# Hybrid retention and HGRN2 layer on eight cores: block 1's x by TensorE, the residual by an accumulating DMA, the sample tile last

## The reference

```python
h = _rmsnorm(x, g_pre)
u = jnp.einsum('btd,de->bte', h, w_in)            # w_in 1024 x 4096
rq, rk, rv, rg, hq, hf, hi, hg = jnp.split(u, cuts.tolist(), axis=-1)   # 512 columns each
rq = _rotary(_heads(rq, RET_HEADS), pos)
rk = _rotary(_heads(rk, RET_HEADS), pos) * (RET_DK ** -0.5)
hq = jax.nn.silu(_heads(hq, HG_HEADS))
f = lb + (1.0 - lb) * jax.nn.sigmoid(_heads(hf, HG_HEADS))
logf, hk = jnp.log(f), 1.0 - f
o_r, o_h, S_ret, S_hg = _run_mixers(S_ret, S_hg, rq, rk, rv, hq, hk, hv, logf, log_gamma)
o = jnp.concatenate([jax.nn.silu(rg) * _merge(_head_norm(o_r)),
                     jax.nn.silu(hg) * _merge(_head_norm(o_h))], axis=-1)
y = jnp.einsum('bte,ed->btd', o, w_out)           # w_out 1024 x 1024
return x + _rmsnorm(y, g_post), S_ret, S_hg
```

## Time and profile before

| | us |
|---|---|
| three runs | 386.45, 387.47, 388.98 |
| median | 387.47 |
| profiled execution | 388.32 |
| its span, slowest core (core 7) | 386.8 |
| span of the fastest core (core 0) | 381.1 |
| PE / DVE / ACT / POOL busy, core 7 | 358.8 / 255.6 / 180.9 / 205.5 |

### The profile page before, as it was taken

How to read it: one execution, slowest core, us unless ns; L and a number is a source line. 1 busy time by engine, 2 the same in 40 slices (tenths; PEclk the granted TensorE clock), 3 DMA queues, 4 the chain that set the end, 5 groups by cost and what they waited for, 6 DMA issues and landing times.

```text
span 386.8 us, 8100 instructions; the slowest of 8 cores (381.1 to 386.8 us)
## 1 busy us (share of the span) xinstructions
PE 358.8 (93%) x2339; PEld 188.1 (49%) x2339; DVE 255.6 (66%) x554; ACT 180.9 (47%) x563; POOL 205.5 (53%) x277
## 2 busy tenths in 40 slices
PE   8599799998988989997999999999999999999982
PEld 8554354455544444453545454545455554554541
DVE  0316565827889998969395949386849467486364
ACT  2431245557767546471636253446262533646341
POOL 8525541545775785774283645375837436347130
PEclk9989899999999999998999999999999999999988
DMA  7999999996488476964537335432233443233217
GB/s 177 204 177 165 202 163 168 178 242 150 87 219 173 157 169 146 231 160 102 153 67 190 88 121 73 164 71 64 55 125 72 133 107 97 110 56 79 101 22 225
DMA packets 64700, 52.62 MB, mean 136 GB/s; under 512 B 45840, under 2 KB 53040, under 8 KB 64656
## 3 DMA queue, kind: packets, MB, share of 16 engines
q1 hardware_dynamic: 59344, 41.61, 42.4%
q0 software_dynamic: 5312, 10.49, 17.7%
HBM read 41.73 MB, written 10.09 MB: 134 GB/s over the span
## 4 chain that ended last, share of the span: by engine, by line
PE 78%; DVE 6%; DMA 5%; issue 3%; POOL 3%; ACT 2%; SPq 1%; DVEq 0%; ACTq 0%; POOLq 0%; another core or an unknown queue 0%
PE bank L671 42%; PE bank L947 14%; PE bank L654 12%; DMA xr<-xp 4%; PE bank L867 2%; PE bank L835 2%; DVE xbf L619 2%; PE bank L872 2%; PE bank L884 2%; POOL QTh L731 1%; DVE fG L713 1%; DVE fR L725 1%; PE bank L934 1%; DMA ogT<-og 1%; SPq L849 1%
## 5 line engine op out<-in xcount | busy, mean ns | idle before, releaser
L671 PE MATMUL bank<-Wi,xT 128*128 128x512 bf16 (+1 forms) x816 | 187.8, 382 | 0.7 <-DVE Sst L889 0.7
L671 PEld LDWEIGHTS bank<-Wi,xT 128*128 128x128 bf16 (+1 forms) x816 | 78.3, 99 | 88.1 <-issue 4.1
L947 PE MATMUL bank<-Wo,ogT 128*128 128x512 bf16 (+1 forms) x272 | 65.1, 391 | 3.6 <-DMA ogT<-og 2.0
L905 DVE SCALAR_TENSOR_TENSOR og<-bank,rsq,gate 128x128 bf16<-128x128 f32 (+1 forms) x136 | 38.6, 343 | 41.2 <-POOL rsq L902 18.3
L654 PE MATMUL bank<-xT,Wi 128*128 128x512 bf16 (+1 forms) x320 | 63.0, 342 | 2.1 <-POOL QTh L731 0.9
L654 PEld LDWEIGHTS bank<-xT,Wi 128*128 128x128 bf16 x320 | 26.9, 98 | 34.2 <-issue 6.9
L947 PEld LDWEIGHTS bank<-Wo,ogT 128*128 128x128 bf16 (+1 forms) x272 | 26.5, 100 | 34.7 <-issue 7.4
L824 POOL TENSOR_TENSOR Sst<-Sst,decS 128x512 f32<-128x512 f32 x30 | 32.9, 1105 | 16.5 <-DVE Sst L889 8.7
L895 ACT ACTIVATE og<-bank 128x128 bf16<-128x128 f32 (+1 forms) x136 | 35.4, 291 | 9.7 <-PE bank L867 6.2
L902 POOL TENSOR_TENSOR rsq<-ssq,mhalf 128x4 f32<-128x4 f32 (+1 forms) x34 | 35.4, 1042 | 5.2 <-POOL ssq L899 0.4
L828 ACT ACTIVATE Sb<-Sst 128x512 bf16<-128x512 f32 x30 | 19.0, 634 | 38.7 <-POOL Sst L824 21.3
(11 more groups left out here) (93 smaller groups left out, 450.8 us busy)
## 6 DMA issues: line engine op xcount, KB each, us to landing
xr<-xp SPq DMA_DIRECT2D x18, 512.0 KB, 4.3
yp<-xr SPq DMA_DIRECT2D x16, 512.0 KB, 2.9
xs<-xp SPq DMA_DIRECT2D x14, 512.0 KB, 5.5
Wi<-w_in POOLq DMA_DIRECT2D x6, 1024.0 KB, 48.5
Wi<-w_in POOLq DMA_DIRECT2D x4, 512.0 KB, 20.3
Wo<-w_out POOLq DMA_DIRECT2D x2, 1024.0 KB, 71.8
rot<-rot_p SPq DMA_DIRECT2D x16, 96.0 KB, 5.0
gpre<-g_pre SPq DMA_DIRECT2D x1, 512.0 KB, 6.7
```

Source lines behind the costliest of these rows:

```text
L671: ins = e.matmul(pb(v)[0:L, :], lhsT=k.xT[:, kc, j * 128:j * 128 + L], rhs=Wi[:, kc, seg * 512:(seg + 1) * 512], start=(kc == 0), stop=(kc ...
L905: S.op(DVE, lambda e, q_=q_, h=h, vo=vo: e.scalar_tensor_tensor(out=ogs[vs][0:L, h * 128:(h + 1) * 128], in0=pb(vo)[0:L, q_ * 128:(q_ + 1) ...
L947: ins = e.matmul(pb(y)[0:L, :], lhsT=ogT[:, kc, 0:L], rhs=Wo[:, kc, n * 512:(n + 1) * 512], start=(kc == 0), stop=(kc == 7))
```

## The change

- Stage A: block 1's four tiles are transposed by PE and ACT as block 0's are. Their first two x loads wait for `("Wi", 5, 3)` instead of `("Wi", 7, 3)`.
- The load of g_post waits for `("Wi", 7, 3)` instead of the first scores.
- Stage E, all prompt tiles but the last: no load into `xr`, no product L954. One DVE instruction per half computes `xr = y * rs2 * gpost`; POOL issues a DMA that adds x from DRAM to `xr` in SBUF; the store on SP follows it.
- The last prompt tile keeps the load and is stored in two halves of 512 columns. The sample tile keeps the load; its product with g_post goes to `tA` in SBUF.
- Program order: all four tiles of block 3, then the sample.
- The planner: a new model of the DMA queues (`Net`), engines start at 900 ns, and each priority gets a random term of up to 500 ns from seed 13. The cost of a POOL instruction with a power as its second operation is added.

```diff
+class Net:
...
+            rate = DMA_RATE if self.t > 12000.0 else DMA_RATE_0
+            rates = [rate] if len(on) == 1 else [rate * (1.0 - HW_SHARE), rate * HW_SHARE]
+            if on[-1][0][2]:
+                rates[-1] = rate / 1.3 if len(on) == 1 else rate * TR_SHARE
...
+        if self.jitter is not None:
+            noise = np.random.RandomState(self.jitter[0]).uniform(-1.0, 1.0, n) * self.jitter[1]
+            for i in range(n):
+                prio[i] += float(noise[i])
...
+                net.issue(fin + (4500.0 if e == POOL else 0.0), e == POOL, o["nbytes"], i, o["tr"])
+                if e != POOL and o["nbytes"] < 120000 and len(net.queues[0]) > 1:
+                    o["lat"] += 3500.0
...
                 elif i < 6:
-                    S.ops[xid]["deps"].add(S.last_w[("Wi", 7, 3)])
+                    S.ops[xid]["deps"].add(S.last_w[('Wi', 5, 3)])
...
-            if (k.b >= 1 and not k.sample):
+            if (k.b >= 2 and not k.sample):
                 S.op(SP, lambda e: e.dma_start_transpose(out=k.xT[:, :, j * 128:(j + 1) * 128], in_=xbf[slot][:, :]),
...
                     for did in late_dma:
-                        S.ops[did]["deps"].add(scid)
+                        S.ops[did]["deps"].add(S.last_w[("Wi", 7, 3)])
...
+            acc = not k.sample and not (k.b == 3 and j == 3)
...
-                S.op(DVE, lambda e, n=n, y=y: e.tensor_tensor(out=pb(y)[0:L, :], in0=pb(y)[0:L, :],
-                                                              in1=gpost[0:L, n * 512:(n + 1) * 512], op=ALU.mult),
-                     reads=[y, "gpost", ("ss2", n)], writes=[y])
+                if not acc:
...
+            if acc:
+                for n in range(2):
+                    S.op(DVE, lambda e, n=n: e.scalar_tensor_tensor(out=xr[slot][0:L, n * 512:(n + 1) * 512], in0=pb(ybk[n])[0:L, :],
+                                                                    scalar=rs2[0:L, 0:1], in1=gpost[0:L, n * 512:(n + 1) * 512],
+                                                                    op0=ALU.mult, op1=ALU.mult),
+                         reads=[ybk[n], "rs2", "gpost"], writes=[("xr", slot) if n == 0 else ("xr1", slot)])
+                S.op(POOL, lambda e: e.dma_start(out=xr[slot][:], in_=xp[t0:t0 + 128, :], accum_op=ALU.add),
+                     reads=[("xr1", slot)], writes=[("xr", slot)], dma_key=("xacc", slot))
...
+            elif not acc:
+                for n in range(2):
+                    stores.append(S.op(SP, lambda e, n=n: e.dma_start(out=yp[t0:t0 + 128, n * 512:(n + 1) * 512], in_=xr[slot][:, n * 512:(n + 1) * 512]),
+                                       reads=[("xr", slot), ("xro", slot, n)], dma_key=("sth", n)))
...
-                for j in range(3):
+                for j in range(4):
...
                     tile(blocks[b], j)
-                front(smp)
-                tile(smp, 0)
-                tile(blocks[b], 3)
+                if 4 == 4:
+                    front(smp)
+                    tile(smp, 0)
...
+        S.jitter = (13, 500.0)
```

More of the change, by code:

```diff
@@ L23 @@
 N_BANKS = 8
-DMA_RATE = 300.0
-SW_RATE = 275.0
-HW_SHARED = 120.0
+DMA_RATE = 310.0
+DMA_RATE_0 = 230.0
+HW_SHARE = 0.45
+TR_SHARE = 0.08
 class Bank:
@@ L144, in estimate_costs @@
             o["port"] = fk.port
+            o["tr"] = o["dma_key"] is not None and o["lat"] < 1500.0
     def bank(self, reserve=0):
@@ L186, in list_schedule @@
                 avail[o["eng"]].append(i)
-        free_t = {e: 0.0 for e in ENGS}
-        sw_free, hw_free, cold = 11500.0, 0.0, 0.0
-        port_free = 0.0
+        free_t = {e: 900.0 for e in ENGS}
+        cold, port_free = 0.0, 0.0
+        net = Net()
         order = {e: [] for e in ENGS}
@@ L197, in free_bank, with landed @@
             return min(fr, key=lambda k: (free_at[k], k))
+        def landed(until):
+            out = net.advance(until)
+            for i, t in out:
+                o = ops[i]
+                t += o["lat"]
+                o["t_land"] = t
+                for sx in succ[i]:
+                    ready_t[sx] = max(ready_t[sx], t + XLAT)
+                    ndeps[sx] -= 1
+                    if ndeps[sx] == 0:
+                        avail[ops[sx]["eng"]].append(sx)
+            return len(out)
         while done < n:
@@ L227, in list_schedule @@
                     best = (e, cand[1], cand[2])
+            if landed(best[2] if best is not None else None):
+                continue
             if best is None:
@@ L280, in list_schedule @@
                     avail[ops[sx]["eng"]].append(sx)
-        self.est_makespan = max(free_t.values())
+        landed(1e9)
+        self.est_makespan = max(max(free_t.values()), max(o.get("t_land", 0.0) for o in ops))
         return order
@@ L960, in stage_E @@
                  reads=["rs2", "mhalf"], writes=["rs2"])
-            for n in range(2):
-                S.op(DVE, lambda e, n=n: e.scalar_tensor_tensor(out=xr[slot][0:L, n * 512:(n + 1) * 512], in0=pb(ybk[n])[0:L, :],
-                                                                scalar=rs2[0:L, 0:1], in1=xr[slot][0:L, n * 512:(n + 1) * 512],
-                                                                op0=ALU.mult, op1=ALU.add),
-                     reads=[ybk[n], "rs2", ("xr", slot)], writes=[("xr", slot)])
@@ new lines, in stage_E @@
+            if k.sample:
+                stores.append(S.op(SP, lambda e: e.dma_start(out=ys[0:16, :], in_=xr[slot][0:16, :]), reads=[("xr", slot), ("xro", slot, 0), ("xro", slot, 1)], dma_key=("sts", 0)))
+                stores.append(S.op(SP, lambda e: e.dma_start(out=ys[16:32, :], in_=xr[slot][32:48, :]), reads=[("xr", slot), ("xro", slot, 0), ("xro", slot, 1)], dma_key=("sts", 1)))
+            elif not acc:
+                for n in range(2):
+                    stores.append(S.op(SP, lambda e, n=n: e.dma_start(out=yp[t0:t0 + 128, n * 512:(n + 1) * 512], in_=xr[slot][:, n * 512:(n + 1) * 512]),
+                                       reads=[("xr", slot), ("xro", slot, n)], dma_key=("sth", n)))
@@ L969, in stage_E @@
             else:
-                stores.append(S.op(SP, lambda e: e.dma_start(out=yp[t0:t0 + 128, :], in_=xr[slot][:]), reads=[("xr", slot)], dma_key=("st", slot)))
+                stores.append(S.op(SP, lambda e: e.dma_start(out=yp[t0:t0 + 128, :], in_=xr[slot][:]), reads=[("xr", slot), ("xr1", slot)], dma_key=("st", slot)))
         def store_state(dst_r, dst_h, tag, Sbuf, kS):
```

72 lines of the change are left out of this document (55 added, 17 removed).

## The result

The changed kernel takes 383.44 us (median of four runs, 382.71 to 384.24) against 387.52 us of the kernel before beside it (386.45 to 388.98): ratio 0.9883, 95% interval 0.9843 to 0.9924. Measured once more with the experiments it took 382.11 us against 387.77, ratio 0.9863 (0.9837 to 0.9889). It is faster by 1.2 to 1.4%. The forecast was 381.6 us. Some executions of every kernel run in a second, slower state, with a lower granted clock on one die or both; times and ratios from here on leave them out.

A forecast was written before the change was run, and what follows sets the result against it. PE was taken as the bound, busy for 93% of the span. 386.8 - 4.8 - 1.2 - 1.1 - 0.6 + 1.8 = 380.9 us of span, 5.9 less, so 387.5 - 5.9 = 381.6 us; range 375 to 388.5.

The forecast's parts named there:

- The middle, -4.8: From 80 to 180 us, 60% of PE's 8.0 us idle time comes back: 4.8 us, between nothing and all.
- The clock, -1.2: At 170 to 180 us on core 7, the lower granted clock costs 1.3 us; removing it brings 1.2 us.
- The rotary table and g_post, -1.1: Early on SP, g_post's 512 KB delay the rotary table DVE and then PE wait for; moving it gains 1.1 us.
- The first 80 us, 0 in the sum: x delays the last part of Wi by up to 3 us, hidden by PE's block 0 work from 60 to 75 us.
- 32 transposes, +1.8: Block 1's four tiles transposed on PE, 0.45 us per 8 transposes, add 1.8 us that count in full.
- Busy times: Sign over the whole span: DVE busy for about 235 us, POOL for 217.
- The accumulation: Stage E's accumulating DMA: 5 us flight, bounds 3.2 to 7.8; issue on POOL 0.80 us each, hidden.
- The rival through SP, 0.14: Stores on SP wait for accumulations, delaying ogT or QKr transposes; 3.3 us per event, four give 394.8 us; chance 0.14.
- The rival "nothing changes": Short chains through DVE and POOL keep the middle's loss; 30% of idle returns, no clock gain, 385.2 us; chance 0.20.
- one of the signs named beforehand: The prediction would be wrong if idle time appeared on PE in 180 to 340 us.
- The end, -0.6: In the last output chain, DVE's state update before L962 goes, 0.6 us; bounds 3.5 us worse, 1.9 better.

The follow-up runs named there:

- old_planner: All operations of the changed kernel, ordered by the planner of before (old DMA model, no random term); ratio 1.0010 to the kernel before.
- seed1: The changed kernel with seed 1 in place of 13 for the planner's random term, same operations; ratio 1.0270 to the kernel before.
- no_x: The changed kernel with block 1's x late and transposed by DMA, g_post after the first scores, order made anew; 385.7 us, ratio 0.9923.
- no_acc: The changed kernel with all tiles loading x and multiplying by g_post on DVE, order made anew; 394.38 us, ratio 1.0163.
- after_again: The changed kernel itself, unchanged, run again beside the fixed-order experiments; 382.11 us, ratio 0.9863 to the kernel before.

## Why the prediction was right, and where it was not

The time fell as forecast: 4.1 us off the median beside it, 5.7 in the second comparison, 5.9 predicted. The terms of the sum did not all hold, and two that were missed nearly cancel: the first 80 us cost PE 1.7 us of idle time, and the end gave back 2.4 us of it where 0.6 had been taken. As means of the eight cores, idle time went by -2.7 (before 22 us), +4.3, -5.3, -0.1 and -2.4 us (from 340 us on), busy time by +0.8 us, the span by -5.3 us.

*The middle, -4.8.* Measured -5.5 us of idle time on core 7 and -5.3 as the mean of the cores. The place and the size were right. The reason was half of it. In this order both parts count: without the early loads the stage is idle for 6.0 us, with DVE's work back for 4.0, against 1.8. But the operations are not enough without the order (old_planner 6.6, seed1 7.4 with the same operations), and so the 7.1 of no_x and 6.0 of no_acc, whose orders are new, don't show by themselves that a part is necessary. The prediction took 60% of the idle "between nothing and all"; the runs show that the order decides between these.

*The clock, -1.2.* The slice that was at 0.84 is at 1.00, and the last sixteen products with Wo, which took 5.31 us, take 3.61 us now. PE's busy time fell by 1.4 us in spite of 32 more transposes. The end thus came out 1.7 us better in that one row, which stood as a bound and not as a term. In the kernel before these products took 4.8 to 5.3 us on six cores and 3.6 on two, in the changed kernel 3.6 on all eight. The slice of 170 to 180 us was at 0.84 on core 7 alone, at 1.00 on the other seven. The row of PE's timeline, core 7:

```profile
370.96 3.61 PE L1009 MATMUL bank<-Wo,ogT 128*48 128x512 bf16 x16
```

*The rotary table and g_post, -1.1.* This step failed, in its reading and in its result. The load of the table that DVE waited for had left SP at 33.94 us, four us ahead of g_post, and took 7.9 us (SP's timeline and the landing, kernel before, core 7):

```profile
33.94 0.33 SPq L984 DMA_DIRECT2D rot<-rot_p  x1
...
DMA to landing us min/median/max: 7.9/7.9/7.9
```

Without g_post such loads take as long: 7.7 us for the one issued at 32.20 us in the changed kernel, 7.8 in old_planner, where DVE still waits for the table on four cores. Nor did DVE's wait reach PE. PE's two waits there end on DVE's L750 of 40.33 us and POOL's L759 of 41.24, which do not need that table, and they stand on core 5 too, where DVE did not wait for it:

```profile
41.16 0.49 PE L1047 MATMUL bank<-ident 128*128 128x128 bf16 x6 [1.15 <-DVE tB L750]
42.65 0.38 PE L774 MATMUL bank<-ident,qtm 128*128 128x128 bf16 x4 [1.00 <-POOL Ktr L759]
```

In the changed kernel g_post leaves after the weights (75.85 us), DVE waits 1.4 us for POOL's sum, and PE 1.2 us at a filler and 1.9 us at L834. The same two waits stand in no_x, where g_post leaves at 36 us: its place was worth nothing to PE, and the chain through POOL costs 0.9 us more than before. DVE's row in the changed kernel:

```profile
40.69 0.69 DVE L810 TENSOR_TENSOR tB<-bank,rot 128x512 f32<-128x512 f32 x1 [1.41 <-POOL Ktr L819]
```

*The first 80 us, 0 in the sum.* Measured +4.5 us of idle time from 22 to 80 and -3.1 before 22 on core 7, together +1.4. The prediction looked at DMA bytes only and named PE's work from 60 to 75 us as the cover. Most of it is not the bytes: on core 7 PE's wait for weights rose from 0.2 to 0.6 us (0.5 to 1.6 on the eight cores, 0 to 1.0 before). The rest came through the order. Where the new planner puts the early norm among block 0's scans, PE waits 2.1 us for the scans and 0.9 us for the first xbf of block 1, 3.0 us of the 8.2; at L834 it waits 0.9 us more than before. The old planner's order with the same early x has 3.5 us of idle time in this stage, so the cost isn't a property of the early x.

*32 transposes, +1.8.* Not seen by itself; nothing speaks against it: PE's mean busy time rose by 0.8 us though the last products became 1.1 us shorter.

*Busy times.* DVE 237.9 us for about 235, POOL 218.7 for 217.

*The accumulation.* Flight 6.1 us for 5, issue 0.94 for 0.80, both within the bounds. The issue stays hidden: POOL is busy for 57%. By the Trainium skill (DMA: Bandwidth & Descriptors, "Anatomy of one DMA") the estimate was 3.2 us; the runs show 4.4 for the plain DMA from POOL and 6.1 for the accumulating one.

*The rival through SP, 0.14.* Its mechanism happened once on two of eight cores, with a load in place of a store: SP stood, a transpose came late, PE waited 2.5 us, without a loss of clock. It had been priced at 3.3 us per event. It made core 7 the slowest of that execution (in after_again the wait was 0.8 us at most), and it was one of the signs named beforehand: idle time in 180 to 340 us. The yp stores did wait for the accumulations, seven times and 23.6 us in all, 6.7 at the longest, but no transpose behind them came too late: after 80 us none of PE's waits on core 7 ends on a DMA.

*The rival "nothing changes".* It is what the same operations give in two of the other orders (0.9984 and 1.0010). It had a chance of 0.20 for short chains "that any order makes anew". A third order (seed 1) loses 2.7%, which no rival named: the prediction had no case in which the order itself makes the kernel slower. The range held the result, but by the draw of the seed.

*The end, -0.6.* This term was mis-sized. Its own step held: on core 7, from the end of the last product with Wo to the end of the span it is 6.6 us against 7.3, -0.7, and DVE's state update no longer stands just ahead of the last L1035. But that is the smallest piece of the end. From the last projection to the end of the span it is 16.8 or 16.9 us on every core, against 21.0 in the mean before. Of these 4.1 us, 2.4 are idle time after 340 us and 1.1 the clock of the last products; the rest is work that the order put elsewhere. The prediction had allowed 1.9 us for the clock, as a bound, and nothing for the idle time. It is not the place of the sample alone: old_planner with the sample last has 16.9 us, but seed1 and no_acc, with the sample last too, have 20.6 and 21.4.

What stays open: how much of the 1.2 to 1.4% is due to the operations. At the order made for them, the early loads are worth at most 11.4 us and DVE's relief about 4.2; with the order redrawn, undoing them gives ratios of 0.9923 and 1.0163. Whether the operations of before have an order as good as this one wasn't tried with more seeds.

## What to carry to other kernels

Where a planner orders the instructions, measure an edit twice: once with the order made anew, and once at a fixed order, by adding or dropping the dependence after planning; only the second prices the edit apart from the order (from above, since the order was made for it), and a few other seeds first tell how much the order alone moves (4% here). A prediction of such a kernel needs the draw of the order as a case of its own, on both sides. On a queue that runs in order, look through each DMA's list of waits for one that it doesn't need: behind a load that lands 2 to 3 us later than usual, it holds everything.

## What the runs showed of the hardware

An accumulating DMA of 512 KB from DRAM to SBUF, issued by POOL, landed in 6.1 us (median of 15, 5.5 to 8.5), the plain one at the same place in the same order in 4.4 (3.6 to 6.8); its issue held POOL for 0.94 us against 0.65. The medians of the other cores are 5.8 to 6.6 and 4.2 to 4.8 us. Of the DMAs beside it two kinds were slower: the transposes QKr from qtm had medians of 3.3 to 4.6 us on the cores of both executions with the adding and of 2.6 to 4.0 without, and the state load took 4.9 to 8.2 us against 3.9 to 5.3. The transposes QKr from Ktr, Kth and ogT were not: 2.4 to 2.8, 2.3 and 3.2 us with it, 2.5 to 2.9, 2.3 to 2.4 and 3.1 to 3.2 without.

The norm instruction of DVE, 128x1024 out of SBUF, takes 1.26 us in two places and 2.21 us in a third:

```profile
74.00 1.26 DVE L679 SCALAR_TENSOR_TENSOR xbf<-xs,rsx,gpre 128x1024 bf16<-128x1024 f32 x1
...
82.60 2.21 DVE L679 SCALAR_TENSOR_TENSOR xbf<-xs,rsx,gpre 128x1024 bf16<-128x1024 f32 x1 [1.18 <-POOL rsx L676]
```

Meanwhile POOL, whose L781 took 1.04 us at 76.68, is stretched too (POOL's timeline, core 7):

```profile
76.68 1.04 POOL L781 TENSOR_TENSOR KTh<-fG 128x512 bf16<-128x512 f32 x1 [0.30 <-DVE fG L773]
...
82.46 1.26 POOL L791 TENSOR_TENSOR QTh<-fQ,fR 128x512 bf16<-128x512 f32 x1
83.68 2.02 POOL L781 TENSOR_TENSOR KTh<-fG 128x512 bf16<-128x512 f32 x1
```

DVE's 2.21 us overlap L791, and L781's first 1.1 us overlap the norm. The Trainium skill (SBUF — State Buffer, "Who interferes with whom") says that a DVE instruction with two inputs in SBUF contends with a GpSimd instruction that reads SBUF; the rows agree with it, and no run tested it.
